# The last prompt block's expert choice, made between the first expert blocks of a one-core diffusion and PEER step

## The reference, cut to what matters

```python
q = (hf @ w_query).reshape(T, N_PEER_HEADS, 2, PEER_KEY_DIM // 2)
s = jnp.einsum('thpk,hpnk->thpn', q, sub_keys)
s1, i1 = lax.top_k(s[:, :, 0], PEER_TOPK)          # 16 of 128 keys, each half
s2, i2 = lax.top_k(s[:, :, 1], PEER_TOPK)
cand = (s1[..., :, None] + s2[..., None, :]).reshape(T, N_PEER_HEADS, 256)
top_s, pos = lax.top_k(cand, PEER_TOPK)            # 16 of 256 pairs
g = jax.nn.softmax(top_s)
a = gelu(einsum('tkd,td->tk', expert_u[ix], hx))   # 8 heads x 16 = 128 experts
out = einsum('tk,tkd->td', gx * a, expert_v[ix])
```

## Time and profile before

| | |
|---|---|
| median of 3 runs | 1884.0 us (1882.87 to 1887.91) |
| the profiled execution | 1883.14 us |
| its span | 1881.3 us, 29902 instructions |
| busy: PE, PEld, DVE, ACT, POOL | 92%, 79%, 81%, 36%, 43% |
| chain that ended last | PE 53%, DVE 26%, issue 13%, DMA 4%, ACT 2% |
| mean granted clock | 0.969 |
| DMA | 520.91 MB, mean 277 GB/s over the span |

### The profile page before, as it was taken

One profiled execution on the slowest core, in us unless ns is written; L12 is line 12 of the kernel. 1 busy time (PEld: TensorE's weight loads), 2 busy tenths in 40 slices (PEclk: granted clock), 3 DMA queues, 4 the chain that ended last, 5 costly groups with the idle time before them and its releaser, 6 DMA issues.

```text
span 1881.3 us, 29902 instructions
## 1 busy us (share of the span) xinstructions
PE 1736.8 (92%) x9942; PEld 1485.8 (79%) x9942; DVE 1519.3 (81%) x3123; ACT 682.8 (36%) x1135; POOL 801.4 (43%) x646
## 2 busy tenths in 40 slices
PE   5799998897899999399999999999999999999994
PEld 2577646447788888389999999999999999999993
DVE  1532127335989899999999999999999999999997
ACT  1222226301367675233333333333333333333332
POOL 1100000000000000278787888887666666666661
PEclk8899989999999999799999999999999999999997
DMA  9434400510044455899999999999999999999993
GB/s 358 150 135 167 162 0 1 239 63 23 1 90 91 90 110 131 284 382 406 403 401 391 407 397 406 404 401 407 407 407 403 397 407 403 397 398 407 407 403 137
DMA packets 253544, 520.91 MB, mean 277 GB/s; under 512 B 113956, under 2 KB 130980, under 8 KB 252198
## 3 DMA queue, kind: packets, MB, share of 16 engines
q1 hardware_dynamic: 178016, 249.00, 37.2%
q0 software_dynamic: 73728, 268.47, 36.1%
q10 hardware_dynamic: 1734, 2.60, 0.4%
HBM read 488.55 MB, written 31.46 MB: 276 GB/s over the span
## 4 chain that ended last, share of the span: by engine, by line
PE 53%; DVE 26%; issue 13%; DMA 4%; ACT 2%; DVEq 1%; POOL 0%; SPq 0%; ACTq 0%; POOLq 0%; PEldq 0%
DVE arena L1190 12%; PE ps L1563 9%; PE ps L1562 9%; PE ps L1561 9%; PE ps L1481 5%; PE ps L1462 4%; PE ps L1532 3%; PE ps L1314 2%; PE ps L1318 2%; PE ps L1315 2%; DMA arena_w<-in_w_mod 2%; DVE V_lo L1140 1%; PE ps L1360 1%; DMA arena_w<-in_w_in 1%; DVE C_lo L1165 1%
## 5 line engine op out<-in xcount | busy, mean ns | idle before, releaser
L1561 PE MATMUL ps<-hT_hi,U_hi 128*128 128x384 f32 x1024 | 344.4, 336 | 13.6 <-DVE U_lo L1135 13.6
L1563 PE MATMUL ps<-hT_hi,U_lo 128*128 128x384 f32 x1024 | 344.5, 336 | 0.0
L1562 PE MATMUL ps<-hT_lo,U_hi 128*128 128x384 f32 x1024 | 343.7, 336 | 0.0
L1561 PE MATMUL ps<-V_hi,C_hi 128*128 128x512 f32 x768 | 299.8, 390 | 18.2 <-DVE C_lo L1165 18.2
L1563 PE MATMUL ps<-V_hi,C_lo 128*128 128x512 f32 x768 | 302.0, 393 | 0.0
L1562 PE MATMUL ps<-V_lo,C_hi 128*128 128x512 f32 x768 | 301.8, 393 | 0.0
L736 ACT CAST V_hi<-V_in 128x1024 fp32r<-128x1024 f32 x128 | 135.0, 1055 | 231.1 <-PE ps L1563 231.1
L475 POOL DMA_INDIRECT arena<-in_expert_u,idxn x128 | 178.5, 1394 | 85.3 <-issue 31.1
L1561 PEld LDWEIGHTS ps<-hT_hi,U_hi 128*128 128x128 f32 x1024 | 192.9, 188 | 18.7 <-issue 13.8
L773 ACT ACTIVATE act_t<-ps 128x384 f32<-128x384 f32 x128 | 63.0, 493 | 394.1 <-PE ps L1563 394.1
L475 POOL DMA_INDIRECT arena<-in_expert_v,idxn x128 | 159.9, 1249 | 94.4 <-DVE arena L1190 42.7
(11 more groups left out here) (231 smaller groups left out, 3230.5 us busy)
## 6 DMA issues: line engine op xcount, KB each, us to landing
U_in<-in_expert_uT SPq DMA_DIRECT2D x128, 512.0 KB, 9.3
V_in<-in_expert_v SPq DMA_DIRECT2D x128, 512.0 KB, 6.5
arena_w<-in_w_mod SPq DMA_DIRECT2D x12, 2048.0 KB, 12.3
gates_scratch<-arena_w SPq DMA_DIRECT2D x6, 4096.0 KB, 20.8
gate_in<-gates_scratch SPq DMA_DIRECT2D x128, 192.0 KB, 7.5
arena_w<-in_w_in SPq DMA_DIRECT2D x4, 2048.0 KB, 8.7
arena_w<-in_w_query SPq DMA_DIRECT2D x1, 7168.0 KB, 20.3
arena_w<-in_w_out SPq DMA_DIRECT2D x2, 2048.0 KB, 10.3
```

Of the source, the lines that this page charges most:

```text
L1561: nc.tensor.matmul(out, hi, rhi, start=start, stop=False)
L1562: nc.tensor.matmul(out, hi, rlo, start=False, stop=False)
L1563: return nc.tensor.matmul(out, lo, rhi, start=False, stop=stop)
```

## The change

The ranking of the last block (block 0, the prompt) stops after three of its four groups. hT_lo and U_lo(0), U_lo(1) follow, and then the fourth group's key_tops, which empties the last score bank. Everything that is left of the choice goes into the slots of blocks 0 to 3 (late_ranking): pair_tops in slot 2, the ranks in 3, the marks and key sums of the first half in 5 and 7, of the second in 9 and 11, the softmax in 13, the clearing of accS in 15. These four blocks handle no gathered row. The 256 dots are spread over the 240 slots of blocks 4 to 63, so that every fifteenth slot has two; these blocks are written out in place of two loops. The additions stay as they were.

Around it: H2s moves out of the arena into free room, and SP issues it ahead of U(2); XF and final_g are issued after gates(2), ahead of U(4); SP's wait for s_acc0 goes. POOL waits also for V and gates of blocks 0 and 1 before its first gather. ACT's Exp for the last block comes after blocks 0 and 1 of the experts. PE's first scores wait only until the score bank of group 2 is empty, and the wait for the last bank comes after them, ahead of scores_u(1).

```diff
@@ -45,6 +45,8 @@
+LATE_PAIRS = 2
+DOT_SLOTS = 8 * (PAIRS // 2 - LATE_PAIRS)
...
-        H2s = cutout(XO + 2 * D, D)
-        h2row = (H2s, H2[0])
+        H2s = gap[:, 0:D]
+        h2row = (H2s, H2[0])
@@ -390,22 +393,21 @@
             for j in range(2):
                 load_v(j, j)
                 load_gates(j, j)
+            sp.wait_ge(s_h2out, 16)
+            sp.dma_start(H2s, h2_d).then_inc(s_h2in, 16)
             sp.wait_ge(s_hTlo, 1)
             sp.wait_ge(s_gev, QUADS * NDEN)
             for n in range(2, 4):
                 sp.wait_ge(s_ulo, n - 1)
                 load_u(n, n % 2)
-            for b in range(NBLK):
-                sp.dma_start(XF[:, b], x1_d[b * P:(b + 1) * P, :]).then_inc(s_xf, 16)
-            sp.dma_start(fing, final_g.unsqueeze(0).broadcast_to([P, D])).then_inc(s_fing, 16)
-            sp.wait_ge(s_acc0, 1)
-            sp.wait_ge(s_h2out, 16)
-            sp.dma_start(H2s, h2_d).then_inc(s_h2in, 16)
             for n in range(2, 4):
                 sp.wait_ge(s_vlo, n - 1)
                 load_v(n, n % 2)
             sp.wait_ge(s_c, 1)
             load_gates(2, 0)
+            for b in range(NBLK):
+                sp.dma_start(XF[:, b], x1_d[b * P:(b + 1) * P, :]).then_inc(s_xf, 16)
+            sp.dma_start(fing, final_g.unsqueeze(0).broadcast_to([P, D])).then_inc(s_fing, 16)
             with sp.Fori(2, PAIRS) as i:
                 for j in range(2):
                     n = i * 2 + j
@@ -487,6 +489,9 @@
+            for j in range(2):
+                pool.wait_ge(s_vin[j], 16)
+                pool.wait_ge(s_gin[j], 16)
             sixteen(expert_u, 0, 0, 0, True)
             with pool.Fori(1, SLOTS // 16) as i:
                 sixteen(expert_u, 0, i, 0)
@@ -735,6 +740,10 @@
+            def gate_exps(n):
+                act.wait_ge(s_top, n + 1)
+                act.activation(top[:, :, :], top[:, :, :], ACT.Exp).then_inc(s_gexp, 1)
-                    if p == QUADS - 4:
-
-                        act.wait_ge(s_top, n + 1)
-                        act.activation(top[:, :, :], top[:, :, :], ACT.Exp).then_inc(s_gexp, 1)
+                    if p == QUADS - 4 and n + 1 < NBLK:
+                        gate_exps(n)
             split_v(0, 0, 1, True)
             experts(0, True, False)
+            gate_exps(NBLK - 1)
             with act.Fori(1, PAIRS // 2) as i:
                 experts(i, False, False)
             dots_gelu(0)
-            def select(n, bd=0, share=(0, 0, 0, 0)):
-
-                b = ORDER[n]
+            def chosen_ranks(n, bd=0):
...
-                    link(dve.tensor_tensor(sel[:, w, :], onehot[:, :, 0], onehot[:, :, 1], ALU.add))
+
+            def chosen_marks(w):
+
+                link(dve.tensor_tensor(onehot, ranks[:, w, :].unsqueeze(2).broadcast_to([P, SLOTS, TOPK]),
+                                       places[:, :].unsqueeze(1).broadcast_to([P, SLOTS, TOPK]), ALU.is_equal))
+                o4 = onehot.rearrange("p (h s) j -> p h s j", h=PH)
+                return note(dve.tensor_tensor(o4, o4, idxf[:, :, w, :].unsqueeze(2).broadcast_to([P, PH, TOPK, TOPK]), ALU.mult))
+
+            def chosen_keys(w, marks):
+
+                dve.wait_ge(s_step, marks)
+                for n_ in (8, 4, 2):
+                    link(dve.tensor_tensor(onehot[:, :, 0:n_], onehot[:, :, 0:n_], onehot[:, :, n_:2 * n_], ALU.add))
+                link(dve.tensor_tensor(sel[:, w, :], onehot[:, :, 0], onehot[:, :, 1], ALU.add))
+
+            def chosen_experts(n):
+
+                b = ORDER[n]
                 dve.tensor_copy(sel1[:, n % 2, :], sel[:, 1, :])
-            def ranking(n, b, bd, keys_share, pairs_share, select_share):
...
+            def select(n, bd=0, share=(0, 0, 0, 0)):
+
+                chosen_ranks(n, bd)
+                for w in range(2):
+                    gate_quads(bd, share[2 * w])
+                    marks = chosen_marks(w)
+                    gate_quads(bd, share[2 * w + 1])
+                    chosen_keys(w, marks)
+                chosen_experts(n)
+
+            def ranking(n, b, bd, keys_share, pairs_share, groups=4):
+                for g in range(groups):
                     key_tops(b, g, bd, keys_share if g else (0,) + keys_share[1:])
                     dve.wait_ge(s_step, steps[0])
                     pair_tops(g, bd, pairs_share)
-                if n + 1 == NBLK:
-
-                    dve.wait_ge(s_hThi, 1)
-                    dve.tensor_tensor(hT_lo[:, :, :], h2T[:, :, P:P + TD], hT_hi[:, :, :].bitcast(f32),
-                                      ALU.subtract).then_inc(s_hTlo, 1)
-                    split_u(0, 0)
-                    split_u(1, 1)
                 dve.wait_ge(s_step, steps[0])
-                select(n, bd, select_share)
             def split_u(n, r):
@@ -1145,10 +1160,45 @@
             dve.tensor_scalar(downb, iota[:, :], -1.0, None, ALU.mult)
             link(dve.memset(onesb, 0.0))
             dve.memset(onesb[0:1, :], 1.0)
-            for n, b in enumerate(ORDER):
+            LAST = NBLK - 1
+            for n, b in enumerate(ORDER[:LAST]):
                 bd = n if 1 <= n <= NDEN else 0
-                ranking(n, b, bd, (1, 2, 1), (0, 1, 1), (2, 2, 2, 3))
+                ranking(n, b, bd, (1, 2, 1), (0, 1, 1))
+                select(n, bd, (2, 2, 2, 3))
                 gate_weights(n)
+            ranking(LAST, ORDER[LAST], 0, (0, 0, 0), (0, 0, 0), 3)
+            dve.wait_ge(s_hThi, 1)
...
+            split_u(0, 0)
+            split_u(1, 1)
+            key_tops(ORDER[LAST], 3)
...
+            def late_ranking(i, q):
+
+                at = 8 * i + q
+                if at == 2:
+                    dve.wait_ge(s_step, steps[0])
+                    pair_tops(3)
+                elif at == 3:
+                    dve.wait_ge(s_step, steps[0])
+                    chosen_ranks(LAST)
+                elif at == 5:
+                    marked[0] = chosen_marks(0)
+                elif at == 7:
+                    chosen_keys(0, marked[0])
+                elif at == 9:
+                    marked[0] = chosen_marks(1)
+                elif at == 11:
+                    chosen_keys(1, marked[0])
+                    chosen_experts(LAST)
+                elif at == 13:
+                    gate_weights(LAST)
+                elif at == 15:
+                    dve.wait_ge(s_gq, QUADS * NDEN)
+                    dve.memset(cutout(XO, 2 * D), 0.0).then_inc(s_acc0, 1)
...
-            def dot_row(k):
-                def go(i, q):
-
-                    if isinstance(i, int) and q == 0:
-                        dve.wait_ge(s_h2in, 16)
-                    dve.wait_ge(s_row[q], 16 * (i + 1))
-                    at = (i - 16 * k) * 8 + q
-                    dst = dots[:, k, at:at + 1] if isinstance(at, int) else dots[:, k, ds(at, 1)]
-                    dve.scalar_tensor_tensor(out=rowr[q], in0=rowr[q], scalar=1.0, in1=h2row[k],
-                                             op0=ALU.mult, op1=ALU.mult, accum_out=dst).then_inc(s_used, 1)
-                return go
+            def dot(r):
+
+                k, q = r // SLOTS, r % RR
+                if r == 0:
+                    dve.wait_ge(s_h2in, 16)
+                dve.wait_ge(s_row[q], 16 * (r // RR + 1))
+                dve.scalar_tensor_tensor(out=rowr[q], in0=rowr[q], scalar=1.0, in1=h2row[k], op0=ALU.mult, op1=ALU.mult,
+                                         accum_out=dots[:, k, r % SLOTS:r % SLOTS + 1]).then_inc(s_used, 1)
+
+            def dot_rows(i, q):
+
+                at = 8 * (i - LATE_PAIRS) + q
+                for r in range(at * 2 * SLOTS // DOT_SLOTS, (at + 1) * 2 * SLOTS // DOT_SLOTS):
+                    dot(r)
                                          op0=ALU.mult, op1=ALU.mult).then_inc(s_y, 1)
             split_v(0, 0)
+            for i in range(LATE_PAIRS):
+                experts(i, False, late_ranking)
+            dve.wait_ge(s_acc0, 1)
             dve.wait_ge(s_gate, NBLK)
-            dve.wait_ge(s_gq, QUADS * NDEN)
-            dve.memset(cutout(XO, 2 * D), 0.0).then_inc(s_acc0, 1)
-            dve.wait_ge(s_acc0, 1)
-            experts(0, False, dot_row(0))
-            with dve.Fori(1, PAIRS // 4) as i:
-                experts(i, False, dot_row(0))
-            with dve.Fori(PAIRS // 4, PAIRS // 2) as i:
-                experts(i, False, dot_row(1))
+            for i in range(LATE_PAIRS, PAIRS // 2):
+                experts(i, False, dot_rows)
             coefs(0)
@@ -1591,9 +1641,10 @@
             pe.wait_ge(s_hTlo, 1)
             pe.wait_ge(s_act2, B2.count("act"))
-            pe.wait_ge(s_dve2, B2.count("dve"))
+            pe.wait_ge(s_dve2, B2.emptied(B2.pos["score", ORDER[-1], 2])[1])
             scores_u(0, 0, True)
             pe.wait_ge(s_gev, QUADS * NDEN)
+            pe.wait_ge(s_dve2, B2.count("dve"))
             experts(0, True, False)
```

(30 more changed lines are left out.)

## The result

The changed kernel takes 1892.3 us, the median of 5 runs (1889.84 to 1896.84), against 1884.0 before (also 5 runs): ratio 1.0043, 95% interval 1.0031 to 1.0055. The forecast was 1875.3 us, with a range from 1864 to 1889: a gain of 8.7 us, where 8.3 were lost.

A forecast was written before the change was run, and what follows sets the result against it. The prediction saw PE as busiest, held early by two waits on DVE and gapless from 830 us. Profiled 1883.14 us - 18.2 (start) + 9.5 (dot half) = 1874.4, plus 0.9 for the median: 1875.3 us, range 1864 to 1889.

The forecast's parts named there:

- The start: Routing to expert block 3: PE starts 6.1 us earlier, sums_v(3) at 807.0 against 825.24, 18.2 us won, bounds 11 and 25.
- the landing of U(4): Ahead of block 2: 13.1 MB issued from 757.6 take 32 us at 410 GB/s, landing about 792; stall 3.9 us.
- the lower clock: PE's restarts after the stalls in blocks 1 and 2: stalls no longer than 4 us, so no clock loss.
- rival 3: First blocks: U(4) lands later, PE idles past 4 us and loses its clock; won 10, not 18: 1883.5 us; chance 0.12.
- The dot half: Blocks 4 to 63: 3.482 MB at 410 GB/s takes 8.49 us a block, 11.3 lost, less 2: 9.5 us.
- the ring: Dot half: rows stand 2 us ahead of use and the ring is full at block 4, so 2 us come off.
- DVE, cost 0: Dot half: sixteen more dots bring DVE's work to 8.19 us a block, under 8.305; cost 0, upper bound 18.
- POOL, inside the DMA term: Dot half: gathers take their short form where DVE waits for rows, nothing added; bounds 0 and 33 us.
- Late code, 0: The 60 written-out dot blocks: late code fetches cost 0; as a rival, two or three landings, about 1900 us, chance 0.03.
- ACT's Exp, 0: Behind expert block 1: the moved Exp brings two table loads, cost 0, as ACT has 314 of 490 us free.
- The add half, 0: The half where rows are added: keeps its pace, nothing of a loss made up and nothing added.
- 14 at 408: Dot half: upper bound of the byte term at 408 GB/s, 60 x 0.23 = 14 us lost; lower bound 0.

The follow-up runs named there:

- e7: The changed kernel with five x loads and final_g put singly between the loads of blocks 4 to 7: 1883.0 us, ratio 0.9993 to the kernel before.
- e1: The changed kernel, loading only a quarter of each gate tile from block 2 on: 1877.7 us, ratio 0.9952 to the kernel before.
- e3: The kernel before, its choice unmoved, with the 256 dots spread over blocks 4 to 63, written out: 1897.63 us, ratio 1.0057.
- e5: The changed kernel without its last 16 dots and their 16 gathers: 1871.2 us, ratio 0.9931 to the kernel before.
- e2: The kernel before with one more plain load of 280 KB in each step of two blocks of the dot half: 1901.85 us, ratio 1.0083.
- e10: The changed kernel with dots from block 1, choice spread in pieces, x loaded at block 68 and behind the last gate tile: 1870.0 us, 0.9926 to the kernel before.
- e9: The changed kernel with C_hi ahead of U_hi on ACT and C_lo ahead of U_lo on DVE: 1882.2 us, ratio 0.9992 to the kernel before.
- e11: e10 with the order of e9 added: 1864.8 us, ratio 0.9903 to the kernel before.
- e4: The changed kernel with x and final_g issued behind the last V load: 1893.9 us, ratio 1.0038 to the kernel before.

## Why the prediction was wrong

**The start: the direction right, 18.2 us forecast, 10.4 measured.** The first product came 8.9 us after the last routing product, 14.7 before: 5.9 us earlier, forecast 6.1. (The routing itself ended 2.3 us later in this execution.) sums_v(1)'s wait was 2.2 us, forecast 3.0. The step that failed is the landing of U(4): "at 410 GB/s, below, 32 us, and with 2 us until the first bytes it lands about 792". It landed at 798.5. The rate was not what failed: from 782 to 798 the queues ran at 411 GB/s, 410 were forecast. But the sum of bytes took all 13.1 MB as waiting in the queue from 757.6 on. The stretch began 2.3 us later, and SP issued V(2) only at 774.6, behind V_lo(0), x from 778.7 on and U(4) at 782.8. So from 765 to 782 the queues moved 325 GB/s, which against 411 is 1.5 MB less, or 3.6 us; together 5.9 of the 6.5. Why they gave no more than 325 at share 0.92 was not taken apart further. So sums_v(2) began at 804.8, not 798.7. PE restarted at the lower clock, which the forecast had put at nothing, and sums_v(3) followed 10.0 us later, not 8.3. That is rival 3's mechanism at rival 3's size ("won 10 instead of 18"); e7 confirms it by giving 9 us back. On DVE's clock the lead at block 4 is 8.9 and not 10.4 us, because Gelu(4) has a table load of 1.28 us ahead of it (815.17) and the product waits for Gelu.

**The dot half: 9.5 us forecast, 16.6 measured, and 1.5 more behind it.** The mechanism was right (the transfers become the bound), and a size was off: "At 410 a block takes 8.49 us". 410 came from windows of 8 us, which showed 408 and 412. Over 490 us no kernel here moved more than 406 GB/s, and 3.482 MB over 8.609 us are 404. By 405 the term is 60 x (8.598 - 8.305) = 17.6, from which the ring takes something, as forecast: PE kept its 8.31 us a block up to sums_v(18) at 939.4 and fell back only behind it, at 406 GB/s. The window of the dot half of before already said 403: the rate's room was 0.5%, the change asked for 4.2%. (That ACT waited 19.3 us for U there is no sign by itself: in e1 it waits 70 us and PE is all but full.) The Trainium skill, "DMA: Bandwidth & Descriptors", section "Where 436 GB/s comes from", gives 435 GB/s for the ports and about 358 for a core's share of HBM, and says that the latter binds such loads. These runs sustain 405, between the two, and the measurement decides: neither figure would have sized the term.

**DVE, cost 0: right**, to 3 us. In e1 it makes the same dots in all but PE's time. **POOL, inside the DMA term: right**, its gathers became shorter on the whole and it waited for DVE. **Late code, 0: right** (e3, e5). **ACT's Exp, 0: right in its cost, wrong in its count**: it brings not two more table loads but 32, of 1.28 us each. The two that were forecast, at 784.8 to 788 us, lie in an ACT that then waits 10 us for U(4), and e5 shows that the 30 in the loop's later steps don't slow the dot half. **The add half, 0**: 1.5 us were lost, and the cause is open. It is not that the queues enter it late: e2 and e3 do so too and lose nothing there (524.0 and 524.2 us, against 524.4 before), and e1 loses 1.1 at 383 GB/s.

**The sum.** - 8.9 + 16.6 + 1.5 for - 18.2 + 9.5: errors of 9.3, 7.1 and 1.5 us, all of one sign. They have no common root: the first is a landing time for which the loads were taken as queued before they could be, with the lower clock behind it, the second a rate that was taken too high. The bound "14 at 408" on the dot half was too narrow for the second reason: both ends came from the short windows. Both signs that the prediction set for being wrong came in, sums_v(3) after 813 (814.8) and a loss of the dot half over 15 (16.6).

## What to carry to other kernels

Work out the bytes of one period and divide by the rate of the longest saturated window, not of the best short one. When that time is within a few per cent of the bounding engine's period, instructions that can move freely by engine time can't move if they carry bytes: here 16 gathers of 0.5 MB cost 17 us when pressed into the last 60 blocks of the dot half (the changed kernel against e5, blocks 8 to 64), and 4 when twelve of them find their place in blocks 1 to 3 (e10 against e5), 2 with the order of e9 besides (e11). For a landing time take each load from the moment at which it can be issued, not the sum of bytes from the start. And ask of every transfer moved in a queue what stands behind it at that moment; the end of a kernel, where the queues run empty, takes what the start has no room for.

## What was not expected of the hardware

- The rate is the same whatever is moved: 3.482 MB a block took 8.603 to 8.632 us in six kernels, with the surplus as gathered rows in five and as a plain load in one. The windows of 490 us of the six show 402 to 406 GB/s.
- A pause of PE of nearly the same length ended once at full and once at half clock: after 2.17 us in the changed kernel the window 788 to 790 shows 1.00, after 2.32 us in e4 too, and after 2.38 us in e1 it shows 0.50 (the first product takes 0.50 us in the first two, 0.80 in e1). After 7.85 us it was 0.50. So the prediction's comparison, a pause no longer than one of 4 us that had kept 0.99, does not make a pause safe. The window of e1:

```profile
788.00:790.00 2.00, 1.77 (x4) 1.48 (x5) 1.97 (x4) 0.03 (x1) 0.00 (x0) 0.50 1.04 412
```
